# One transformer layer and one hybrid layer on one core: retention's norm moved into the next pair's attention, and the waits around six hand-overs reordered

## What is computed

```python
# first block
n = rms_norm(h, attn_norm_w);  aq, ak, av, rq, rk, rv, rg = split(n @ w_in)
y_attn = windowed_gqa_sink(rope(rms_norm(aq)), rope(rms_norm(ak)), av, sink)     # 8 heads of 64, window 128
ret    = rms_norm(bidirectional_retention(rope(rq), rope(rk) * 64**-.5, rv), ret_norm_w)   # 8 heads of 64
h = h + concat(y_attn, silu(rg) * ret) @ w_out
m = rms_norm(h, ffn_norm_w);  h = h + (silu(m @ w_gate) * (m @ w_up)) @ w_down
# second block; shifts, scales and gates come from silu(c) @ w_ada + b_ada
x = x + 0.5 * g1 * swiglu(rms_norm(x) * (1 + sc1) + sh1)
z = (rms_norm(x) * (1 + sc2) + sh2) @ w_mix + b_mix
y_a = sigmoid(o) * rms_norm(mlstm(silu(causal_conv(q, k)), v, i, f))   # 4 heads, causal, gated
y_b = forgetting_attention(rms_norm(q), rms_norm(k), v, f)             # 16 heads of 64, causal
x = x + g2 * ((sigmoid(g_a) * (y_a @ w_branch_a) + sigmoid(g_b) * (y_b @ w_branch_b)) @ w_out)
x = x + 0.5 * g3 * swiglu(rms_norm(x) * (1 + sc3) + sh3)
```

## Time and profile before

| | |
|---|---|
| median of 3 runs | 2117.44 us (2114.41 to 2117.54) |
| profiled execution, its own time | 2117.74 us |
| its span, first to last instruction | 2115.8 us |
| mean granted TensorE clock | 0.985 |
| PE busy | 96% of the span |
| DVE, ACT, POOL busy | 41%, 37%, 36% |
| DMA | 30.8% of 16 engines, 99 GB/s read |

### The profile page before, as it was taken

One profiled execution on the slowest core, in us unless ns is written; L12 is line 12 of the kernel. 1 busy time (PEld: TensorE's weight loads), 2 busy tenths in 40 slices (PEclk: granted clock), 3 DMA queues, 4 the chain that ended last, 5 costly groups with the idle time before them and its releaser, 6 DMA issues.

```text
span 2115.8 us, 27569 instructions
## 1 busy us (share of the span) xinstructions
PE 2036.8 (96%) x9466; PEld 1598.8 (76%) x9466; DVE 863.2 (41%) x1242; ACT 772.8 (37%) x1176; POOL 770.7 (36%) x310
## 2 busy tenths in 40 slices
PE   7998999999999999989979999999999999999999
PEld 5666677888887788878857776776788877888887
DVE  4665565343223534343375554444321164222200
ACT  5334343322322333222235564556522243332211
POOL 2212134444443444444423332222244444444443
PEclk9999999999999999999999999999999999999999
DMA  4211134553322455542212221111123332333322
GB/s 146 55 46 41 49 90 159 198 189 100 111 96 81 140 197 191 189 172 95 88 40 70 70 73 45 53 56 50 60 90 98 92 96 72 97 99 94 103 95 94
DMA packets 56639, 210.70 MB, mean 100 GB/s; under 512 B 6289, under 2 KB 7057, under 8 KB 56593
## 3 DMA queue, kind: packets, MB, share of 16 engines
q1 hardware_dynamic: 55440, 208.71, 30.8%
q10 hardware_dynamic: 1152, 1.38, 0.2%
HBM read 207.96 MB, written 2.10 MB: 99 GB/s over the span
## 4 chain that ended last, share of the span: by engine, by line
PE 70%; issue 22%; POOL 5%; DVE 2%; ACT 1%; POOLq 0%; ACTq 0%; DVEq 0%
PE bank L423 62%; POOL wlo L368 4%; PE bank L686 1%; PE bank L740 1%; PE bank L755 1%; PE bank L766 1%; PE bank L450 1%; PE bank L775 1%; DVE xl L1372 0%; DVE ssum L1347 0%; DVE sqn L1366 0%; POOL wlo L373 0%; PE bank L472 0%; POOL xl L379 0%; PE bank L747 0%
## 5 line engine op out<-in xcount | busy, mean ns | idle before, releaser
L368 POOL TENSOR_TENSOR wlo<-raw,whi 128x1024 fp32r<-128x1024 f32 (+1 forms) x290 | 738.6, 2547 | 1260.5 <-ACT whi L842 1260.5
L423 PE MATMUL bank<-xh,whi 128*128 128x512 f32 x1688 | 684.4, 405 | 36.5 <-DVE xl L1357 13.5
L423 PE MATMUL bank<-xh,wlo 128*128 128x512 f32 x1688 | 663.0, 393 | 0.0
L423 PE MATMUL bank<-xl,whi 128*128 128x512 f32 x1688 | 662.8, 393 | 0.0
L842 ACT ACTIVATE whi<-raw 128x1024 fp32r<-128x1024 f32 (+1 forms) x298 | 330.3, 1108 | 649.4 <-PE bank L423 624.9
L423 PEld LDWEIGHTS bank<-xh,whi 128*128 128x128 f32 x1688 | 320.3, 190 | 119.1 <-issue 19.6
L423 PEld LDWEIGHTS bank<-xl,whi 128*128 128x128 f32 x1688 | 320.4, 190 | 69.4 <-issue 7.0
L423 PEld LDWEIGHTS bank<-xh,wlo 128*128 128x128 f32 x1688 | 319.8, 189 | 68.6
L423 PE MATMUL bank<-acth,whi 128*128 128x512 f32 x528 | 209.8, 397 | 7.1 <-POOL wlo L368 7.1
L423 PE MATMUL bank<-actl,whi 128*128 128x512 f32 x528 | 209.4, 397 | 0.0
L423 PE MATMUL bank<-acth,wlo 128*128 128x512 f32 x528 | 209.3, 396 | 0.0
(11 more groups left out here) (312 smaller groups left out, 2045.9 us busy)
## 6 DMA issues: line engine op xcount, KB each, us to landing
raw<-w_dram SPq DMA_DIRECT2D x250, 512.0 KB, 3.6
adaw<-ada_dram SPq DMA_DIRECT2D x72, 512.0 KB, 4.4
raw<-wd_dram SPq DMA_DIRECT2D x48, 704.0 KB, 4.1
h<-x_dram SPq DMA_DIRECT2D x4, 512.0 KB, 7.3
out_dram<-h SPq DMA_DIRECT2D x8, 256.0 KB, 4.1
rel<-rel_dram ACTq DMA_DIRECT2D x1, 513.0 KB, 6.4
crow<-c_dram SPq DMA_DIRECT2D x1, 512.0 KB, 3.4
gates_raw<-gates_dram SPq DMA_DIRECT2D x1, 384.0 KB, 9.3
```

Of the source, the lines that this page charges most:

```text
L368: nc.gpsimd.tensor_tensor(wlo[:, s, 0:width], raw[:, s, 0:width], whi[:, s, 0:width].bitcast(F32), ALU.subtract).then_inc(sem("w_lo"), 1)
L423: mm = nc.tensor.matmul(proj[b][:], w[:, s, W], v[:, k, :], start=first and j == 0 and a == 0, stop=last and j == len(chunks) - 1 and a == ...
```

## The change

In the order of the program: the constants' eight DMAs go from ACT to SP, behind the loads of x; the first two loads of `down1` go between the last loads of `load_ada`; the last chunk's squares are no longer added into `ssum` on DVE but summed by a second matmul into the same PSUM bank (`norm_sum_last`), and `norm_sum` goes one chunk forward; the first scores of the next pair go ahead of the end of the fourth `ret` slab, and with them the exponentials, maxima and scalings of its first block go ahead of the gate's SiLU; the sum, roots and output of retention's norm go into block 0 of the next step (`ret_sum`, `ret_roots`, `ret_out`), and for the last step into the first `out` slab; the evacuation of the attention's values goes ahead of the last rope; the split of slab 3 goes from chunk 7 to chunk 5; `conv_tile` goes ahead of `place_rows(0)`; in the first forgetting pair the second sum goes forward into the slab and the scores go ahead of its last two chunks, with ACT's value evacuation and split behind the exponentials. For this, step 0 is written out apart from the loop on ACT and DVE.

```diff
+            def load_down(run, i, k):
+                load(i * 2 + (SLAB[f"down{run}"] + k), k % 2,
+                     wd_in[bass.ds(i * 2 + (run * N_DOWN + k), 1)].rearrange("a p n -> (a p) n"), DC)
...
             load_x(3)
+            for dst, at, n in ((blk, P, P), (rot, 2 * P, P), (sin, 5 * P + S, S), (cos, 5 * P, S), (ident, 0, P), (ge, 3 * P, P),
+                               (leconst, 4 * P, P)):
+                sp.dma_start(dst[:], const_in[:, at:at + n]).then_inc(sem("const_in"), 16)
+            sp.dma_start(rel[:], rel_in).then_inc(sem("rel_in"), 16)
...
                 for s in range(4):
+                    if s > 1:
+                        load_down(1, i, s - 2)
                     load_ada(i, 4 * ADA0 + 4 * (FC // 2 - 1), s)
-            down_loop(1)
+            down_loop(1, first=1)
...  # PE
             def norm_sum(r):
-                pe.wait_ge(sem("ssum"), primed(KC * (r + 1)))
-                nc.tensor.matmul(bank[6][:], ones[:], ssum[:], start=True, stop=True).then_inc(sem("norm_sum"), 1)
+                pe.wait_ge(sem("ssum"), primed((KC - 1) * (r + 1)))
+                nc.tensor.matmul(bank[6][:], ones[:], ssum[:], start=True, stop=False, skip_group_check=True)
+            def norm_sum_last(r):
+                pe.wait_ge(sem("sq"), KC * (r + 1))
+                nc.tensor.matmul(bank[6][:], ones[:], sqn[:, (KC - 1) % 2, :], start=False, stop=True,
+                                 skip_group_check=True).then_inc(sem("norm_sum"), 1)
...
-                        if k == 3:
+                        if k == 2:
                             norm_sum(r)
...
+                        if k == 4:
+                            norm_sum_last(r)
...
                 if b == 0:
-                    pe.wait_ge(sem("y_lo"), primed(t * 2))
+                    if t > 0:
+                        pe.wait_ge(sem("y_lo"), primed(t * 2 - 1))
+                        pe.wait_ge(sem("ret_ln"), t)
...
+            def ret_sum(t):
+                pe.wait_ge(sem("y_lo"), primed(t * 2 + 1))
+                pe.wait_ge(sem("ret_sq"), t + 1)
+                nc.tensor.matmul(bank[7][:], blk[:], rsq[:], start=True, stop=True).then_inc(sem("ret_ss"), 1)
...
+                    elif b == 0:
+                        wide("ret", t, 4, 0, part=(0, 4))
+                        if t > 0:
+                            ret_sum(t - 1)
+                        wide("ret", t, 4, 0, part=(4, KC))
...
-                wide("ret", t, 4, 3, part=(5, KC))
                 if more:
                     win_scores(t + 1, 0)
+                wide("ret", t, 4, 3, part=(5, KC))
                 ret_cross(t)
-                pe.wait_ge(sem("ret_sq"), t + 1)
-                nc.tensor.matmul(bank[7][:], blk[:], rsq[:], start=True, stop=True).then_inc(sem("ret_ss"), 1)
...
-            for s, lo, hi in ((0, 0, KC - 1), (1, 0, KC // 2), (0, KC - 1, KC), (1, KC // 2, KC)):
+            for s, lo, hi in ((0, 0, 2), (0, 2, KC - 1), (1, 0, KC // 2), (0, KC - 1, KC), (1, KC // 2, KC)):
+                if (s, lo) == (0, 2):
+                    ret_sum(AH // 2 - 1)
...
-            wide("fox", 0, 6, 2)
+            wide("fox", 0, 6, 2, part=(0, 2))
             fox_sums(0, 0, 1, 1)
+            wide("fox", 0, 6, 2, part=(2, 6))
             pe.wait_ge(sem("f_rows"), 4)
             fox_scores(0, 0, 0)
+            wide("fox", 0, 6, 2, part=(6, KC))
...  # ACT
+            def ret_roots(t):
+                act.wait_ge(sem("ret_ss"), t + 1)
+                inverse_root("ret", t, bank[7][:], rr[:], DH)
...
                         win_exps(t, 2 * b + 3)
+                    if b == 0 and tail:
+                        ret_roots(t - 1)
...
+                if more:
+                    win_exps(t + 1, 0)
+                    win_exps(t + 1, 1)
                 act.preload_act_table(ACT.Silu)
                 act.wait_ge(sem("evac1"), primed(t * 2 + (TILE["ret"] // 2 + 2)))
                 nc.scalar.activation(rsil[:], rsil[:], ACT.Silu).then_inc(sem("ret_sil"), 1)
                 split(t, 4, n, 5, WC)
                 act.preload_act_table_set("natural_log_exp_and_others")
-                if more:
-                    win_exps(t + 1, 0)
-                    win_exps(t + 1, 1)
                 act.wait_ge(sem("ret_values"), t + 1)
                 nc.scalar.activation(rsq[:], bank[4][:], ACT.Square).then_inc(sem("ret_sq"), 1)
-                act.wait_ge(sem("ret_ss"), t + 1)
-                inverse_root("ret", t, bank[7][:], rr[:], DH)
...
-            FF_SPLITS = {0: 0, KC - 1: 1}
+            FF_SPLITS = {0: 0, 5: 1}
...
+            conv_tile(0, 1, 0, 1)
             act.wait_ge(sem("rows_clear"), 3)
             place_rows(0, msM, slice(0, MH), "m_rows")
-            conv_tile(0, 1, 0, 1)
             place_rows(1, msm, slice(0, MH), "m_rows")
...
             fox_roots(0, 0)
-            fox_values(0, 2)
             fox_roots(0, 1)
-            split(0, 6, SLAB["fox"], 4, WC)
             fox_exps(0, 0)
             fox_exps(0, 1)
+            fox_values(0, 2)
+            split(0, 6, SLAB["fox"], 4, WC)
...  # DVE; ret_out(t) holds the four instructions that ended a step before
                     if b == 0:
                         ret_decay_logs(t)
+                        if tail:
+                            ret_out(t - 1)
...
                 ret_scans(t)
-                ret_tile(t, 3)
                 if more:
                     win_maxima(t + 1, 0)
                     win_maxima(t + 1, 1)
                     win_scale(t + 1, 0)
                     win_scale(t + 1, 1)
+                ret_tile(t, 3)
...
+                if p == QT - 1:
+                    att_scaled(p + 1)
+                    win_scale(0, 1)
                 normed_rope(p, qall[:, p - 1, :] if p else kf[:])
-                att_scaled(p + 1)
-                if p == QT - 1:
-                    win_scale(0, 1)
+                if p < QT - 1:
+                    att_scaled(p + 1)
```

More of the change, by code:

```diff
@@ L299, in wide_loop, with down_loop @@
                         load_wide(i, 2, n0, k)
-            def down_loop(run):
-                n0 = SLAB[f"down{run}"]
-                with sp.Fori(0, N_DOWN // 2) as i:
+            def load_down(run, i, k):
+                load(i * 2 + (SLAB[f"down{run}"] + k), k % 2,
+                     wd_in[bass.ds(i * 2 + (run * N_DOWN + k), 1)].rearrange("a p n -> (a p) n"), DC)
+            def down_loop(run, first=0):
+                with sp.Fori(0, N_DOWN // 2 - first) as i:
                     for k in range(2):
-                        load(i * 2 + (n0 + k), k,
-                             wd_in[bass.ds(i * 2 + (run * N_DOWN + k), 1)].rearrange("a p n -> (a p) n"), DC)
+                        load_down(run, i, 2 * first + k)
             def load_x(c):
@@ L624, in _ @@
                     norm_sum(0)
+                    norm_sum_last(0)
                     wide("att", 0, 2, 0, ready=("z_lo", 0), part=(KC - 1, KC))
@@ L1596, in _ @@
             dve.wait_ge(sem("ret_consts"), 12)
-            with dve.Fori(0, AH // 2 - 1) as t:
-                mixing_step(t)
+            mixing_step(0, tail=False)
+            with dve.Fori(0, AH // 2 - 2) as i:
+                mixing_step(i + 1)
             mixing_step(AH // 2 - 1, more=False)
+            ret_out(AH // 2 - 1)
             def scale_of(r):
@@ L1605, in scale_of, with add_tile @@
                 return lambda m: scl[:, bass.ds(m + (r - 2) * KC, 1)] if not isinstance(m, int) else scl[:, m + (r - 2) * KC:m + (r - 2) * KC + 1]
-            def add_tile(name, per, r, gate, i, s):
+            def add_tile(name, per, r, gate, i, s, last=False):
                 m = i * 2 + s
@@ L1619, in add_tiles @@
                     clear_sum(r)
-                with dve.Fori(0, KC // 2) as i:
+                with dve.Fori(0, KC // 2 - 1) as i:
                     for s in range(2):
                         add_tile(name, per, r, gate, i, s)
+                add_tile(name, per, r, gate, KC // 2 - 1, 0)
+                add_tile(name, per, r, gate, KC // 2 - 1, 1, last=True)
             def ff_product(run, i, i0, jj):
```

50 lines of the change are left out of this document (26 added, 24 removed).

## The result

The changed kernel takes 2094.54 us (median of 4 runs, 2092.97 to 2095.44), the kernel before 2116.80 beside it: a ratio of 0.9896, with the interval 0.9879 to 0.9913. Its profiled execution took 2094.88 us, with a span of 2093.1. The forecast was 2099 with the range 2092 to 2107: right in sign and, in the main, in mechanism; 4.5 us too slow.

A forecast was written before the change was run, and what follows sets the result against it. PE, busy for 96% of the span, was taken as the bound, leaving its waits and low-clock matmuls to win; eight parts summed to 18.9 us, 2117.7 to 2098.8, given as 2099, range 2092 to 2107.

The forecast's parts named there:

- The steps: Three mixing-step hand-overs: sum's wait goes, 2.2 us wait comes at block 1; gain 6.9, less 2.5 for clock, net 4.4.
- the start: Start of the kernel: one more float32 matmul at the low clock, partly returned; loss 0.6 us, bounds 0 and 1.3.
- the forgetting pair: First forgetting pair: new gap of 2.05 us at the second sum, wide slab sooner; gain 2.6 us.
- `out`: Last step into `out`: PE waits 1.75 us for the square after two chunks, instead of 3.15; gain 3.7 us.
- the norms: Norm sums, r = 1 to 4: wait for last addition goes, 3.3 us; split at chunk 5, 1.1; sum 4.4.
- the mLSTM: `conv_tile` ahead of gate rows: 10.3 us gap moves to slab 4; net loss 0.9, bounds loss 1.8 to gain 2.
- the rope: Values ahead of last rope: first transposes wait about 5 us for the rope; loss 2.8 us, bounds 1.6 and 3.3.
- rival B: Everything hidden: clock stays at 2.4 GHz in all places, DVE's row chain isn't held; 2092 us, chance 0.14.
- Rival A: Retention chain moves its wait on: over 4 us idle at block 1 in each step; 2106 us, chance 0.16.
- D: A wait left in place holds the other parts too, so steps start where they did; 2110 us, chance 0.06.
- Rival C: Slower: new gap at block 1 leaves PE at 1.2 GHz for the rest of each step; 2143 us, chance 0.04.
- `down1`: First `down1` matmul: earlier load removes the 7.08 us gap and its low clock; gain 8.1 us, bounds 6 and 8.3.

The follow-up runs named there:

- run 9: Changed kernel with DVE's scalings of block 1 put ahead of `ret_out`'s four instructions in the three hand-overs: 2091.93 us, ratio 0.9880 against the kernel before.
- run 8: Changed kernel with the eight constants' loads issued by ACT behind chunk 5 of the start again, not by SP: 2095.29 us, ratio 0.9905 against the kernel before.
- Runs 2: Changed kernel with DVE's old order of last rope, values' evacuation and second scaling put back: 2095.61 us, ratio 0.9901 against the kernel before.
- 5: Changed kernel with the down slabs' loads for `down1` issued behind the last loads of the vector again: 2104.05 us, ratio 0.9951 against the kernel before.
- runs 7: Changed kernel with ACT's second split of a hand-over at chunk 7 again: 2094.29 us, ratio 0.9902 against the kernel before.
- 11: Changed kernel with scalings ahead of `ret_out`, first head's value tiles ahead of the rows, old rope order, split at chunk 7: 2079.44 us, ratio 0.9827.
- run 12: As 11, and for the first mLSTM head ACT copies values and rows ahead of SiLU and makes the first two weights earlier: 2076.55 us, ratio 0.9803.
- run 6: Changed kernel with all eight squares added by DVE and summed by one matmul again, split still at chunk 5: 2101.36 us, ratio 0.9937 against the kernel before.
- the repetition: The changed kernel run once more without any edit: 2096.34 us, ratio 0.9904 against the kernel before.
- run 10: Changed kernel with ACT evacuating and splitting the first head's two value tiles ahead of the `place_rows` they stood behind: 2092.08 us, ratio 0.9888.

## Why the prediction was right, and where it was off

By place the gain is 3.5 us more than forecast (22.4 less 18.9). The steps give 4.2 us more, the start 1.5, the forgetting pair 0.4 and `out` 0.3; the norms (1.5), the mLSTM (0.8) and the rope (0.6) give less than forecast. The last us between 3.5 and 4.5 lies in what the places leave out (the spans differ by 22.7, the time around them by 0.1) and in comparing a median with a profiled execution. The result, 2094.5, is nearer to rival B (2092, everything hidden) than to the forecast: B's condition on the clock held at block 1, its condition on DVE's row chain did not. Rival A needed over 4 us of wait at block 1 and found 1.7; D needed the steps to start where they did, and the wait for the rope held nothing else back.

**Steps (part 1).** Mechanism right: no wait at the sum, a new one at block 1, released by DVE's scaling, with the four instructions of `ret_out` as its cause (run 9 took it away with them). It was 1.66, 1.65 and 1.32 us, forecast 2.2. The term that was mis-sized is the clock: half of the low-clock price was charged for each step, 2.5 us in all, and the stretches behind all three waits are at 1.00. The other 1.7 us are the waits, shorter than counted. The stretches (columns as in the earlier trace rows):

```profile
125.83:129.83 4.00, 4.00 (x25) 2.81 (x26) 2.60 (x8) 1.77 (x5) 0.00 (x0) 1.00 0.00 0
170.53:174.53 4.00, 4.00 (x25) 2.81 (x26) 2.61 (x8) 1.77 (x5) 0.00 (x0) 1.00 0.00 0
214.94:218.94 4.00, 4.00 (x25) 2.81 (x26) 2.55 (x8) 1.85 (x5) 0.00 (x0) 1.00 0.02 4
```

Over the nine profiled kernels that have these waits, 26 of 27 stretches stayed at 1.00; one fell to 0.56 (run 8, first step). The Trainium skill ("TensorE: Matmul & The Clock Gate", section "A second HAM failure mode: psum-queue depth-cycling") tells of a kernel in which short idle times between groups of matmuls made the clock swing between its two levels. By that all three would have paid; the trace disagrees for these waits of 1.3 to 1.7 us. Rival C needed 13 us of low clock a step; there is none.

**`out`, rope, `down1`, forgetting pair (2, 3, 5, 7).** 4.0, -3.4, 8.1 and 3.0 against 3.7, -2.8, 8.1 and 2.6, with the waits at 1.65, 5.08, 0.46 and 2.00 us against 1.75, about 5, "within 1" and 2.05. Runs 2 and 5 confirm two of them by undoing them.

**Norms (4).** The total for r = 1 to 4 was forecast 4.4 and is 2.9. Step that failed: the split at chunk 5, credited with 1.1 us, costs 1.7 to 2.6 (runs 7, 11 and 12), and at r = 1 it made a wait of 2.09 us for slab 4 that the prediction doesn't have. The square's part, 3.3, was too small: run 6 gives 5.6 by place, 1.6 of it low clock at r = 1, so 4.0 without. The two errors nearly cancel, which is luck and would never have shown in the whole time.

**Ahead of the mLSTM (6).** The credit of nothing for the largest gap was right, and the reason too: `arow` now takes 2.67 us [0.68 in rows 8], and slab 4 waits 10.05.

```profile
1073.88 2.67 DVE L1828 TENSOR_TENSOR arow<-zi,cs 4x512 f32<-4x512 f32 x1
```

The loss is 2.2 by place, forecast 0.9. The stretch at 1.2 GHz behind the gap was taken as the eight matmuls of the old one; here it lasts for some fourteen (the 6 us from 1091.85 are at 0.50, by 0.427 us each). In the repetition it is 2 us shorter, and the loss 1.1. So the order was priced rightly, and the rest is where the low clock ended.

**Start (8).** Forecast a loss of 0.6, found a gain of 0.9. The summing matmuls start at 22.02 instead of 22.70 and are 1.38 and 1.02 us long instead of 2.08, since the clock rises sooner:

```profile
22.02 1.38 PE L442 MATMUL bank<-ssum,ones 128*128 128x512 f32 x2
23.24 1.02 PE L446 MATMUL bank<-sqn,ones 128*128 128x512 f32 x2
```

In run 12, whose start is the same program, they are longer, and the gain of 0.9 us is gone:

```profile
22.23 1.91 PE L442 MATMUL bank<-ssum,ones 128*128 128x512 f32 x2
23.93 1.25 PE L446 MATMUL bank<-sqn,ones 128*128 128x512 f32 x2
```

Ten runs (all but 6 and 8) have this start unchanged, and the slab that starts at 36.55 in the changed kernel starts from 1.0 us sooner to 0.9 us later in them. The granted clock over the 4 us from 18.00 is 1.00 in run 10, 0.67 in the changed kernel and 0.50 in run 12. So the 0.9 is where the clock happened to rise, and neither the gain nor the forecast loss of 0.6 can be told from it.

## What to carry to other kernels

Where one engine issues an order for several chains, a wait moves to the next instruction in that order whose data is late; look for which copies stand in line with their data long there, and move those (runs 9, 10 and 12 together gave 12 us by place, more than any one part of the change), instead of exchanging which slab waits. Undo each part by itself and compare by place: in this change one part of about 3 us (the rope), one of 1.7 to 2.6 (the split) and one of 1 to 2 (the rows) were losses inside a gain of 22. And charge a low clock only where rows at the same kind of gap show it, in all of the trace: the kernel before also had low stretches behind waits of only 1.8 us for a chunk (0.57 over the 4 us from 330.76 and from 706.00), which the prediction didn't weigh.

## What was not expected of the hardware

The granted clock behind a gap of a given length isn't given by the program. Thirteen profiled executions have the same wait of 2.00 us at the first forgetting pair with the same matmuls around it: in five the 3 us behind it are at 1.00, in eight at 0.50 to 0.74, and each of the eight pays 1.6 us. Ahead of slab 4 at r = 1, behind full slabs, waits of 1.4 to 2.2 us kept the clock in seven kernels, behind 2.25 it fell partly in one (0.85 over 2 us), and behind 2.60 and 2.62 it fell in both (0.62 and 0.65). The length isn't all of it: 12 us ahead of these, PE waits 1.8 to 1.9 us for a chunk in all thirteen, and within the 4 us behind that the clock is low in ten. The two with the long waits are of the three that kept it there. So single terms of the comparison by place are sure only to about 1.6 us wherever a gap of some 2 us stands, and terms smaller than that need a second kernel that shows them too. This also is why the profile of one program may differ from its next by as much as a part of a change is worth.
